# Reordering the ScalarE and VectorE work of pair 3 in the first MLP product

## The chip, the cores and the metric

The kernel is one program on one core of a Trainium2 chip, in float32 throughout (the matrix products are made of rounded parts, see below). The metric is the device time of one execution in microseconds (us), lower is better. The engines are called as in the profile: PE (TensorE), ACT (ScalarE), DVE (VectorE), POOL (GpSimd) and SP (SyncE, which only issues transfers here). Each engine works through its own list of instructions in the order in which the program gives them, and waits at a semaphore until it has reached the number asked for.

## The reference, cut to what matters

The reference is one layer of a diffusion trunk: a norm, a combined projection, a mixer, an output projection, and then an MLP, over 1024 tokens of width 1024. The change touches only the MLP's first product and its squared ReLU:

```python
D_MODEL = 1024
D_FF = 4 * D_MODEL
h2 = modulate(x, norm2_w, sh2, sc2)
return x + g2 * (jnp.square(jax.nn.relu(h2 @ w_mlp1)) @ w_mlp2)
```

## The kernel before, in words

**The tiling.** The 4096 hidden features are 32 tiles of 128, taken two at a time as 16 pairs, 0 to 15. Pairs 0 and 1 are multiplied plainly. From pair 2 on a pair is a 2 by 2 block product, two rows of 128 features by two halves of 512 tokens, with the contraction cut in two, and is made with 7 block products in place of 8. Weights and activations are combined by sums and differences before, and the results after. Each block product is 12 matmuls of 128x128 by 128x512: four tiles of the contraction, each with rounded weights by rounded activations, rounded weights by the rest of the activations, and the rest of the weights by rounded activations.

**PE.** `hidden_products(i, odd)` makes the seven products of pair i in the order `HID_ORDER = (0, 5, 2, 1, 4, 3, 6)`. I call them product 1 to product 7 of the pair by their place in this order. They go into three PSUM accumulators: A (in `ob`), B and C (in `sm`). Product 1 fills A. Product 3 goes on adding to A, so the content of A has to be copied out before it (first copy). Product 5 adds to A again (second copy before it). Product 4 begins C anew, and product 6 adds to C (third copy between them). Product 7 adds to A after DVE's second addition has read it.

**ACT, the weight parts.** `w1_high(pair, n, b)` writes the rounded weights for product n+1 of the pair, one 128x512 instruction at L1882 (`slot<-raw` or `slot<-held`); `held` and two quarters of `raw` come from POOL's sums.

**DVE, the weight parts.** `w1_low(pair, n, b)` subtracts the rounded weights from the exact ones (L2534), and PE waits for it at each product.

**POOL.** `part_sums1` makes four sums for each pair (L889, L891, L894, L897), each held up by a count of `w1_low`: the fourth one, L897, of the pair waits until `w1_low(pair, 3)` is done, since it overwrites `held`, and the first one, L889, of the next pair waits for `w1_low(pair, 5)`.

**The way out of the banks.** `copy_out(i, odd, n, ...)` on ACT (L1941) copies an accumulator to the buffer `hid`. `add_out` on DVE (L2596) adds another accumulator to what was copied: the first addition adds B, the second adds A after product 5, and `third_out` adds C after product 6 and applies the squared ReLU. On ACT, `first_out` and `next_out` make the squared ReLU (L1910 and L1912) behind the first and second addition, and `last_block` makes it from A after product 7.

**The staged parts for the second product.** The squared hidden blocks of a pair are combined by DVE (`t_made`, L2568 to L2582, four of them in a row of dependences), rounded by ACT (`t_high`, L1936, seven for each pair), their rest made by DVE (`t_low`, L2589, seven for each pair), and stored to HBM by SP (`keep_hidden`, L709). Stage buffers are used again by the next pair, so `t_high` waits for the store of the pair before.

**What sets the order.** The order is written out by hand. Pair 2, and the staged parts of pairs 0 and 1, are a straight list ahead of the function `period(i, odd, kind)`, which is the list for one pair from 3 to 15, on ACT and on DVE. Within it, work of pair i (weight parts, copies, additions) is mixed with the staged parts of pair i-1. Only `period(3, 1)` is touched by the change; pairs 4 to 13 are a loop over the same function.

The semaphores that the prediction speaks of: `hid_prod` counts PE's products, `y_copied` the copies, `y_added` the additions, `w1_lo` the weight rests. PE's waits ahead of a product are these:

```python
if j in (2, 4, 3):
    pe.wait_ge(y_copied, i * 3 + {2: -5, 4: -4, 3: -3}[j])
if j == 6:
    pe.wait_ge(y_added, i * 3 - 4)
```

Of the kernel before, what the change touches and what calls it, by code (L numbers as in the profile page):

```python
# [64 lines left out]
NPART = 7  # L65
# [141 lines left out]
def hybrid_trunk(nc, wstream, wg_in, wm1, wm2, xt, ct, small_in, gw_in, out):  # L207
    ctx = ExitStack()
    with ctx:
# [1277 lines left out]
        def _(act):  # L1487
# [426 lines left out]
            def last_block(pair, odd):  # L1914

                act.wait_ge(hid_prod, pair * NPART - NPART)
                relu_squared(odd, 1, 0, pair * 3 - 3, hid_bank(ACC_A, odd))
# [20 lines left out]
            def copy_out(i, odd, n, acc, at, row, half):  # L1938

                act.wait_ge(hid_prod, i * NPART + (at + 1 - 2 * NPART))  # L1940
                act.activation(hid_block(odd, row, half), hid_bank(acc, odd), ACT.Copy).then_inc(y_copied, 1)  # L1941

            def first_out(i, odd):
                act.wait_ge(y_added, i * 3 - 5)
                relu_squared(odd, 0, 0, i * 3 - 5)

            def next_out(i, odd):
                act.wait_ge(y_added, i * 3 - 4)
                relu_squared(odd, 1, 1, i * 3 - 4)
# [27 lines left out]
            t_high(0, 0, 6, "first")  # L1977
            w1_high(2, 5, 0, True)
            w1_high(2, 6, 0, True)
            for j in T_ORDER[:2]:  # L1980
                t_high(1, 1, j, "plain")
            first_out(2, 0)
            act.wait_ge(t_lo, NPART)
            copy_out(2, 0, 1, ACC_A, 2, 0, 1)
            copy_out(2, 0, 2, ACC_C, 3, 1, 1)
            w1_high(3, 0, 1)
            w1_high(3, 1, 1)
# [1 line left out]
            t_high(1, 1, 2, "plain")  # L1989
            t_high(1, 1, 5, "plain")  # L1990
            t_high(1, 1, 4, "plain")
            t_high(1, 1, 6, "plain")
            next_out(2, 0)
            for j in T_ORDER[:2]:
                t_high(2, 0, j)

            def period(i, odd, kind=""):

                prev, old, new = i - 1, 1 - odd, 1 - odd
                last = kind == "last"  # L2000
                w1_high(i, 2, odd)
                last_block(prev, old)
                act.wait_ge(t_sum, i * 4 - 7)
                act.wait_ge(t_lo, i * NPART + (T_AT[0] + 1 - 2 * NPART))
                copy_out(i, odd, 0, ACC_A, 0, 0, 0)
                w1_high(i, 3, odd)
                t_high(prev, old, 1)
                t_high(prev, old, 2)
                w1_high(i, 4, odd)
                t_high(prev, old, 5)  # L2010
                first_out(i, odd)
                act.wait_ge(t_lo, i * NPART + (T_AT[4] + 1 - 2 * NPART))
                copy_out(i, odd, 1, ACC_A, 2, 0, 1)
                w1_high(i, 5, odd)
                t_high(prev, old, 4)
                copy_out(i, odd, 2, ACC_C, 3, 1, 1)
                w1_high(i, 6, odd)
                t_high(prev, old, 6)
                if last:
                    w2_high(0, 0, 0, True)  # L2020
                    w2_high(0, 0, 1, True)
                else:
                    w1_high(i + 1, 0, new)
                next_out(i, odd)
                if not last:
                    w1_high(i + 1, 1, new)
                for j in T_ORDER[:2]:
                    t_high(i, odd, j, "last" if last else "")
                if last:
                    t_high(i, odd, 1, "last")  # L2030
                    w2_high(0, 0, 2, True)

            period(3, 1)
            with act.Fori(2, 7) as q:
                period(q * 2, 0)
                period(q * 2 + 1, 1)
# [57 lines left out]
        def _(dve):  # L2094
# [554 lines left out]
            t_made(1, 1, 4, "plain")  # L2649
            t_low(1, 1, 5)  # L2650
            t_low(1, 1, 4)
            t_low(1, 1, 6)
            third_out(2, 0)
            for j in T_ORDER[:2]:
# [2 lines left out]
            def period(i, odd, kind=""):  # L2657

                prev, old, new = i - 1, 1 - odd, 1 - odd
                last = kind == "last"  # L2660
                w1_low(i, 2, odd)
                for n in (1, 2, 3):
                    t_made(prev, old, n)
                w1_low(i, 3, odd)
                t_low(prev, old, 1)
                add_out(i, odd, 0, ACC_B, 1, 0, 0)
                w1_low(i, 4, odd)
                t_low(prev, old, 2)
                t_made(prev, old, 4)
                w1_low(i, 5, odd)  # L2670
                t_low(prev, old, 5)
                w1_low(i, 6, odd)
                t_low(prev, old, 4)
                add_out(i, odd, 1, ACC_A, 4, 1, 1)
                if last:
                    w2_low(0, 0, 0)
                else:
                    w1_low(i + 1, 0, new)
                t_low(prev, old, 6)
                third_out(i, odd)  # L2680
                if last:
                    t_low(i, odd, 0, kind)
                    t_made(i, odd, 1)
                    t_low(i, odd, 3, kind)
                else:
                    w1_low(i + 1, 1, new)
                    for j in T_ORDER[:2]:
                        t_low(i, odd, j)

            period(3, 1)  # L2690
            with dve.Fori(2, 7) as q:
                period(q * 2, 0)
                period(q * 2 + 1, 1)
# [180 lines left out]
```

## Time and profile before

| what | value |
|---|---|
| device time, median of 3 runs | 1073.67 us |
| lowest and highest of the 3 | 1072.82 and 1074.81 us |
| the profiled execution, device time | 1072.9 us |
| its span, first to last instruction | 1071.1 us |
| PE busy in the span | 1051.0 us, 98% |
| DVE busy in the span | 812.7 us, 76% |
| mean granted TensorE clock | 0.997 of full speed |

The span is 1.8 us shorter than the time of the same execution. Busy shares are means over the whole program; the stretch that the change touches is about 40 us long, from 480 to 521 us after the span's start. A row of the timeline gives the start, the duration, the engine, the source line, the operation and its tiles, how many instructions are merged in the row, and in brackets how long the engine had been idle before it and what ended that.

### The profile page before, as it was taken

To read this page: it belongs to the slowest core of one execution; us is meant where nothing else is said; L and a number is where in the kernel's file an instruction comes from. 1 tells how busy PE (TensorE), PEld (TensorE's weight loads), DVE (VectorE), ACT (ScalarE), POOL (GpSimd) and SP (SyncE) were. 2 spreads that over 40 slices of the span, in tenths; PEclk is the share of its full clock that TensorE was granted. 3 is DMA by queue.
4 is the path that set the end of the run, shared out by engine and by line. 5 is a ranking of instruction groups with operands and counts; after the bars stand their busy time and mean duration, and the time that the engine had idled before them with its cause. 6 is when DMAs were issued, how large, how long until landed. Compare 5 with 4: busy or idle time off the path is not lost.

```text
span 1071.1 us, 16432 instructions
## 1 busy us (share of the span) xinstructions
PE 1051.0 (98%) x5566; PEld 849.9 (79%) x5566; DVE 812.7 (76%) x1069; ACT 515.3 (48%) x833; POOL 273.6 (26%) x268
## 2 busy tenths in 40 slices
PE   7999999999999999999999999999999999999996
PEld 4688888777788888887888888888788888888884
DVE  5878868656546864899887787878988777787776
ACT  6665444357526233676667666666422222222234
POOL 1000006586101000012423323233422231222223
PEclk9999999999999999999999999999999999999998
DMA  9623331101013871226876675768755854774604
GB/s 350 254 90 127 118 118 40 41 21 40 28 53 117 308 278 62 79 98 249 321 265 246 232 272 222 273 235 307 302 192 202 352 219 176 311 282 177 246 1 157
DMA packets 66646, 199.82 MB, mean 187 GB/s; under 512 B 5664, under 2 KB 15136, under 8 KB 66592
## 3 DMA queue, kind: packets, MB, share of 16 engines
q1 hardware_dynamic: 66592, 199.11, 49.3%
q8 instruction: 33, 0.54, 0.2%
q14 instruction: 21, 0.17, 0.0%
HBM read 139.32 MB, written 59.77 MB: 186 GB/s over the span
## 4 chain that ended last, share of the span: by engine, by line
PE 48%; DVE 5%; DMA 1%; issue 1%; ACT 0%; POOL 0%; SPq 0%; DVEq 0%; ACTq 0%; POOLq 0%
PE main L1457 13%; PE ob L1415 12%; PE sm L1415 9%; PE sm L1457 8%; PE ob L1457 6%; DVE stage L2589 1%; DMA hidden_kept<-stage 1%; DVE XR L2707 1%; DVE XR L2779 1%; DVE slot L2539 0%; DVE slot L2534 0%; DVE t_tmp L2573 0%; DVE stage_last L2589 0%; DVE hid L2596 0%; DVE h_sum L2545 0%
## 5 line engine op out<-in xcount | busy, mean ns | idle before, releaser
L1415 PE MATMUL ob<-h_sum,slot 128*128 128x512 f32 x504 | 121.5, 390 | 2.3 <-ACT hid L1941 1.8
L957 PE MATMUL main<-a_hi,w_hi 128*128 128x512 f32 x376 | 123.0, 408 | 0.0
L1894 ACT ACTIVATE slot<-raw 128x512 fp32r<-128x512 f32 x80 | 50.1, 631 | 148.5 <-PE main L1457 58.4
L957 PE MATMUL main<-a_lo,w_hi 128*128 128x512 f32 x376 | 116.4, 391 | 0.0
L957 PE MATMUL main<-a_hi,w_lo 128*128 128x512 f32 x376 | 116.1, 390 | 0.0
L1415 PEld LDWEIGHTS ob<-h_sum,slot 128*128 128x128 f32 x504 | 94.3, 188 | 23.1 <-DVE slot L2534 2.9
L2707 DVE SCALAR_TENSOR_TENSOR XR<-main,small,XR 128x512 f32<-128x512 f32 x112 | 83.3, 750 | 28.8 <-PE main L1457 27.7
L957 PEld LDWEIGHTS main<-a_lo,w_hi 128*128 128x128 f32 x376 | 70.6, 188 | 15.5
L957 PEld LDWEIGHTS main<-a_hi,w_lo 128*128 128x128 f32 x376 | 70.6, 188 | 15.3
L957 PEld LDWEIGHTS main<-a_hi,w_hi 128*128 128x128 f32 x376 | 67.0, 188 | 15.8 <-issue 2.9
L1457 PE MATMUL main<-t_even,slot 128*128 128x512 f32 x336 | 78.1, 389 | 0.0
L2534 DVE TENSOR_TENSOR slot<-raw,slot 128x512 fp32r<-128x512 f32 x70 | 62.9, 900 | 17.6 <-ACT slot L1882 17.6
L1415 PE MATMUL sm<-h_hi,slot 128*128 128x512 f32 x224 | 73.5, 389 | 0.0
L1457 PEld LDWEIGHTS main<-t_even,slot 128*128 128x128 f32 x336 | 63.1, 188 | 13.1
L889 POOL TENSOR_TENSOR held<-raw 128x512 f32<-128x512 f32 x14 | 23.0, 1642 | 183.5 <-DMA raw<-wstream 136.2
L838 POOL TENSOR_TENSOR scaled_state<-tst,decay 64x128 f32<-64x128 f32 x60 | 28.5, 475 | 144.6 <-ACT tst L1623 140.1
L2539 DVE TENSOR_TENSOR slot<-raw,slot 128x512 fp32r<-128x512 f32 x80 | 59.8, 763 | 1.9 <-ACT slot L1894 1.9
L2707 DVE SCALAR_TENSOR_TENSOR XR<-sm,small,XR 128x512 f32<-128x512 f32 x64 | 47.7, 748 | 13.0 <-PE sm L1457 12.1
L1894 ACT ACTIVATE slot<-part_sum 128x512 fp32r<-128x512 f32 x32 | 20.2, 631 | 64.4 <-POOL part_sum L921 29.2
L918 POOL TENSOR_TENSOR raw<-part_sum,raw 128x512 f32<-128x512 f32 x16 | 21.3, 1332 | 115.2 <-DVE slot L2539 115.2
L2707 DVE SCALAR_TENSOR_TENSOR XR<-ob,small,XR 128x512 f32<-128x512 f32 x48 | 35.7, 749 | 17.8 <-PE ob L1457 17.7
L1415 PEld LDWEIGHTS sm<-h_hi,slot 128*128 128x128 f32 x224 | 42.0, 188 | 8.7
(341 smaller groups left out, 2401.6 us busy)
## 6 DMA issues: line engine op xcount, KB each, us to landing
hidden_kept<-stage SPq DMA_DIRECT2D x98, 512.0 KB, 4.5
raw<-wstream SPq DMA_DIRECT2D x60, 512.0 KB, 4.3
t_even<-hidden_kept SPq DMA_DIRECT2D x56, 512.0 KB, 5.5
raw<-wstream SPq DMA_DIRECT2D x16, 1024.0 KB, 5.7
stage<-hidden_kept SPq DMA_DIRECT2D x21, 512.0 KB, 5.1
stage_last<-hidden_kept SPq DMA_DIRECT2D x21, 512.0 KB, 6.0
wmod<-wm SPq DMA_DIRECT2D x8, 1024.0 KB, 11.7
mbuf<-wm SPq DMA_DIRECT2D x16, 512.0 KB, 4.1
```

Source lines behind the costliest of these rows:

```text
L838: pool.tensor_tensor(scaled_state[DK:P, :], tst[DK:P, h % 2, c, :], decay[DK:P, h, c:c + 1].broadcast_to([DK, DV]), ALU.mult).then_inc(sta ...
L889: pool.tensor_tensor(sums, a21, a22, ALU.add).then_inc(w1_sum, 1)
L918: pool.tensor_tensor(a11, sums, a11, ALU.subtract).then_inc(w2_sum, 1)
L957: ins = pe.matmul(main[:, bank, half * HALF:(half + 1) * HALF], w[:, slot, k, :], x[:, half * HALF:(half + 1) * HALF], start=begin, stop=end)
L1415: ins = pe.matmul(hid_bank(acc, odd), slots1[j][:, w, kp, :], parts[x][:, kp, :], start=PARTS[j][3] and kp == 0 and m == 0, stop=kp == KP ...
L1457: ins = pe.matmul(product_bank(s, acc, q), slots2[j][:, w, q, kp, :], tset[odd][j][kp][:, x, :], start=begins and kp == 0 and n == 0, stop ...
L1894: act.activation(slots2[j][:, 0, :, :, :], operand(s, j), ACT.Copy).then_inc(w2_hi, 1)
L2534: tt(slots1[j][:, 1, :, :], operand1(b, j), slots1[j][:, 0, :, :].bitcast(F32), ALU.subtract).then_inc(w1_lo, 1)
L2539: tt(slots2[j][:, 1, :, :, :], operand(s, j), slots2[j][:, 0, :, :, :].bitcast(F32), ALU.subtract).then_inc(w2_lo, 1)
L2589: tt(y[:, 1, :], sources(odd)[j], y[:, 0, :].bitcast(F32), ALU.subtract).then_inc(t_lo, 1)
L2707: stt(out=XR[m][:, cols], in0=product_bank(s, acc, q), scalar=mods[:, 3, m:m + 1], in1=XR[m][:, cols], op0=ALU.mult, op1=ALU.add).then_inc ...
L2779: stt(out=XR[k][:, cols], in0=bank(4 + n), scalar=one_col("fw", k), in1=XR[k][:, cols], op0=ALU.mult, op1=ALU.mult).then_inc(out_made, 1)
```

## The change

On ACT, in the list for pair 2, the second copy of pair 2 goes ahead of one staged part and of `first_out(2)`. Still ahead of `period(3, 1)`, the third and fourth weight parts of pair 3 and its first copy are put in: the third weight part ahead of the last staged part of pair 1, the first copy ahead of `next_out(2)`, the fourth weight part ahead of the first staged parts of pair 2. In `period(3, 1, "begun")` the fifth weight part and the second copy of pair 3 stand directly behind `last_block`, ahead of three staged parts and `first_out(3)`.

On DVE, the third weight rest of pair 3 goes ahead of the last staged rest of pair 1. Within the period the fourth and fifth weight rests each stand where the third and fourth stood. The weight rest for product 1 of pair 4 moves ahead of a staged rest and of pair 3's second addition. PE, POOL and SP have the same lists as before. All other pairs keep their order. No instruction is added or taken away.

```diff
             w1_high(2, 6, 0, True)
-            for j in T_ORDER[:2]:
-                t_high(1, 1, j, "plain")
-            first_out(2, 0)
+            t_high(1, 1, T_ORDER[0], "plain")
             act.wait_ge(t_lo, NPART)
             copy_out(2, 0, 1, ACC_A, 2, 0, 1)
+            t_high(1, 1, T_ORDER[1], "plain")
+            first_out(2, 0)
             copy_out(2, 0, 2, ACC_C, 3, 1, 1)
...
             t_high(1, 1, 4, "plain")
+            w1_high(3, 2, 1)
             t_high(1, 1, 6, "plain")
+            act.wait_ge(t_sum, 5)
+            act.wait_ge(t_lo, NPART + T_AT[0] + 1)
+            copy_out(3, 1, 0, ACC_A, 0, 0, 0)
             next_out(2, 0)
+            w1_high(3, 3, 1)
             for j in T_ORDER[:2]:
                 t_high(2, 0, j)
...
+                if kind == "begun":
+                    last_block(prev, old)
+                    w1_high(i, 4, odd)
+                    second_copy()
+                    t_high(prev, old, 1)
+                    t_high(prev, old, 2)
+                    t_high(prev, old, 5)
+                    first_out(i, odd)
...
-            period(3, 1)
+            period(3, 1, "begun")
...
             t_low(1, 1, 4)
+            w1_low(3, 2, 1)
             t_low(1, 1, 6)
...
-                w1_low(i, 2, odd)
+                begun = kind == "begun"
+                w1_low(i, 3 if begun else 2, odd)
                 for n in (1, 2, 3):
                     t_made(prev, old, n)
-                w1_low(i, 3, odd)
+                w1_low(i, 4 if begun else 3, odd)
                 t_low(prev, old, 1)
                 add_out(i, odd, 0, ACC_B, 1, 0, 0)
-                w1_low(i, 4, odd)
+                if not begun:
+                    w1_low(i, 4, odd)
...
                 w1_low(i, 6, odd)
+                if begun:
+                    w1_low(i + 1, 0, new)
                 t_low(prev, old, 4)
                 add_out(i, odd, 1, ACC_A, 4, 1, 1)
```

The order on ACT from the last staged parts of pair 1 to the first addition's squared ReLU of pair 3, before. `slot1_2`, `slot1_1`, `slot1_4` are the third, fourth and fifth weight part, `hid1<-ob` at L1941 is the first copy and then the second, `stage` are staged parts.

```order
L1936 ACTIVATE stage6_161<-t_tmp_140 128x512
L1910 ACTIVATE hid0_134<-hid0_134 128x512
L1912 ACTIVATE hid0_134<-hid0_134 128x512
L1936 ACTIVATE stage0_155<-hid0_134 128x512
L1936 ACTIVATE stage3_158<-hid0_134 128x512
L1882 ACTIVATE slot1_2_143<-raw1_1_192 128x512
L1910 ACTIVATE hid0_134<-ob 128x512
L1912 ACTIVATE hid0_134<-hid0_134 128x512
L1941 ACTIVATE hid1_135<-ob 128x512
L1882 ACTIVATE slot1_1_142<-held_137 128x512
```

The same place on ACT with the change, up to the second copy:

```order
L1882 ACTIVATE slot1_2_143<-raw1_1_192 128x512
L1936 ACTIVATE stage6_161<-t_tmp_140 128x512
L1941 ACTIVATE hid1_135<-ob 128x512
L1910 ACTIVATE hid0_134<-hid0_134 128x512
L1912 ACTIVATE hid0_134<-hid0_134 128x512
L1882 ACTIVATE slot1_1_142<-held_137 128x512
L1936 ACTIVATE stage0_155<-hid0_134 128x512
L1936 ACTIVATE stage3_158<-hid0_134 128x512
L1910 ACTIVATE hid0_134<-ob 128x512
L1912 ACTIVATE hid0_134<-hid0_134 128x512
L1882 ACTIVATE slot1_4_145<-raw1_1_192 128x512
L1941 ACTIVATE hid1_135<-ob 128x512
```

The first copy (first L1941 row of each) had eight of these instructions ahead of it and has two now, the last staged part of pair 1 and the third weight part. The second copy (last row) stands ahead of the staged parts 1, 2 and 5 of pair 2, which it followed before.

The order on DVE in the period of pair 3, before, from the fourth weight rest to the second addition. `hid1<-hid1,sm` is the first addition, `hid1<-hid1,ob` the second, `slot1_0<-raw1_0` the first weight rest of pair 4.

```order
L2534 TENSOR_TENSOR slot1_1_142<-held_137,slot1_1_142 128x512
L2589 TENSOR_TENSOR stage1_156<-t_tmp_140,stage1_156 128x512
L2596 TENSOR_TENSOR hid1_135<-hid1_135,sm 128x512
L2534 TENSOR_TENSOR slot1_4_145<-raw1_1_192,slot1_4_145 128x512
L2589 TENSOR_TENSOR stage2_157<-t_tmp_140,stage2_157 128x512
L2582 TENSOR_TENSOR t_tmp_140<-hid0_134,t_tmp_140 128x512
L2534 TENSOR_TENSOR slot1_3_144<-held_137,slot1_3_144 128x512
L2589 TENSOR_TENSOR stage5_160<-hid0_134,stage5_160 128x512
L2534 TENSOR_TENSOR slot1_6_147<-raw1_1_192,slot1_6_147 128x512
L2589 TENSOR_TENSOR stage4_159<-hid0_134,stage4_159 128x512
L2596 TENSOR_TENSOR hid1_135<-hid1_135,ob 128x512
L2534 TENSOR_TENSOR slot1_0_141<-raw1_0_191,slot1_0_141 128x512
```

The same place on DVE with the change, from the fifth weight rest (L2552 is the weight rests' line there, L2607 the staged rests', L2614 the additions', L2600 the fourth difference's):

```order
L2552 TENSOR_TENSOR slot1_4_145<-raw1_1_192,slot1_4_145 128x512
L2607 TENSOR_TENSOR stage1_156<-t_tmp_140,stage1_156 128x512
L2614 TENSOR_TENSOR hid1_135<-hid1_135,sm 128x512
L2607 TENSOR_TENSOR stage2_157<-t_tmp_140,stage2_157 128x512
L2600 TENSOR_TENSOR t_tmp_140<-hid0_134,t_tmp_140 128x512
L2552 TENSOR_TENSOR slot1_3_144<-held_137,slot1_3_144 128x512
L2607 TENSOR_TENSOR stage5_160<-hid0_134,stage5_160 128x512
L2552 TENSOR_TENSOR slot1_6_147<-raw1_1_192,slot1_6_147 128x512
L2552 TENSOR_TENSOR slot1_0_141<-raw1_0_191,slot1_0_141 128x512
L2607 TENSOR_TENSOR stage4_159<-hid0_134,stage4_159 128x512
L2614 TENSOR_TENSOR hid1_135<-hid1_135,ob 128x512
```

All three weight rests `slot1_2`, `slot1_1` and `slot1_4` now stand ahead of the first addition, where two of them stood; ahead of the second addition the first weight rest of pair 4 has come in.

## Rows read from the trace of the kernel before

**Rows 1.** The page's busy time (share of the span) and instructions, two engines.

```profile
PE 1051.0 (98%) x5566; PEld 849.9 (79%) x5566; DVE 812.7 (76%) x1069; ACT 515.3 (48%) x833; POOL 273.6 (26%) x268
```

**Rows 2.** Busy time by stretch: start:end us, length, engines' busy time, clock, DMA.

```profile
core 0: us, PE busy (x) PEld busy (x) DVE busy (x) ACT busy (x) POOL busy (x), PEclk, DMA share, GB/s
479.92:499.56 19.64, 19.30 (x86) 15.69 (x85) 19.61 (x23) 12.38 (x22) 7.66 (x4) 1.00 0.53 214
499.56:521.00 21.44, 19.52 (x85) 15.45 (x84) 20.64 (x31) 16.39 (x31) 6.60 (x4) 1.00 0.91 323
521.00:540.04 19.04, 19.04 (x86) 15.77 (x85) 15.82 (x25) 13.27 (x25) 6.33 (x4) 1.00 0.76 273
```

**Rows 3.** Timeline of PE, pairs 3 and 4: starts of products.

```profile
502.27 0.39 PE L1415 MATMUL sm<-h_hi,slot 128*128 128x512 f32 x1
...
506.92 3.00 PE L1415 MATMUL ob<-h_sum,slot 128*128 128x512 f32 x12 [1.76 <-ACT hid L1941]
...
518.28 3.00 PE L1415 MATMUL ob<-h_sum,slot 128*128 128x512 f32 x12 [0.16 <-DVE hid L2596]
...
529.28 2.88 PE L1415 MATMUL sm<-h_sum,slot 128*128 128x512 f32 x12
```

**Rows 4.** The chain of work that ended last, in pair 3: start, us, what.

```profile
504.01 8.94 DMA hidden_kept<-stage
...
517.54 0.61 DVE hid L2596
```

**Rows 5.** Timeline of ACT, pair 3 and one row of pair 4.

```profile
501.76 0.64 ACT L1936 ACTIVATE stage<-t_tmp 128x512 fp32r<-128x512 f32 x1 [1.33 <-DVE t_tmp L2582]
...
506.19 0.58 ACT L1941 ACTIVATE hid<-ob 128x512 f32<-128x512 f32 x1
...
510.50 0.63 ACT L1910 ACTIVATE hid<-hid 128x512 f32<-128x512 f32 x1 [0.73 <-DVE hid L2596]
...
511.71 0.58 ACT L1941 ACTIVATE hid<-ob 128x512 f32<-128x512 f32 x1
512.19 0.62 ACT L1882 ACTIVATE slot<-held 128x512 fp32r<-128x512 f32 x1
513.02 0.63 ACT L1936 ACTIVATE stage<-hid 128x512 fp32r<-128x512 f32 x1 [0.22 <-DMA hidden_kept<-stage]
...
529.48 0.60 ACT L1941 ACTIVATE hid<-ob 128x512 f32<-128x512 f32 x1 [0.60 <-PE ob L1415]
```

**Rows 6.** Timeline of DVE, pair 3.

```profile
505.98 0.69 DVE L2534 TENSOR_TENSOR slot<-raw,slot 128x512 fp32r<-128x512 f32 x1
...
507.37 0.69 DVE L2573 TENSOR_TENSOR t_tmp<-hid,t_tmp 128x512 f32<-128x512 f32 x1
...
508.58 0.68 DVE L2534 TENSOR_TENSOR slot<-held,slot 128x512 fp32r<-128x512 f32 x1
...
509.79 0.68 DVE L2596 TENSOR_TENSOR hid<-hid,sm 128x512 f32<-128x512 f32 x1
510.38 1.19 DVE L2534 TENSOR_TENSOR slot<-raw,slot 128x512 fp32r<-128x512 f32 x1
...
512.84 0.69 DVE L2534 TENSOR_TENSOR slot<-held,slot 128x512 fp32r<-128x512 f32 x1
...
514.70 1.14 DVE L2534 TENSOR_TENSOR slot<-raw,slot 128x512 fp32r<-128x512 f32 x1 [0.56 <-ACT slot L1882]
515.76 1.78 DVE L2589 TENSOR_TENSOR stage<-hid,stage 128x512 fp32r<-128x512 f32 x1
517.46 0.68 DVE L2596 TENSOR_TENSOR hid<-hid,ob 128x512 f32<-128x512 f32 x1
```

**Rows 7.** Timeline of POOL, the sums of pairs 3 and 4.

```profile
509.41 1.61 POOL L897 TENSOR_TENSOR held<-raw 128x512 f32<-128x512 f32 x1 [11.25 <-DVE slot L2534]
513.61 1.68 POOL L889 TENSOR_TENSOR held<-raw 128x512 f32<-128x512 f32 x1 [2.58 <-DVE slot L2534]
515.36 1.63 POOL L891 TENSOR_TENSOR raw<-raw 128x512 f32<-128x512 f32 x1
```

More of the change, by code:

```diff
@@ L2000, in period, with second_copy @@
                 last = kind == "last"
[L2001 to L2013, printed above, removed]
+                def second_copy():
+                    act.wait_ge(t_lo, i * NPART + (T_AT[4] + 1 - 2 * NPART))
+                    copy_out(i, odd, 1, ACC_A, 2, 0, 1)
+                if kind == "begun":
[6 more added lines that the diff above has]
+                    first_out(i, odd)
+                else:
+                    w1_high(i, 2, odd)
+                    last_block(prev, old)
+                    act.wait_ge(t_sum, i * 4 - 7)
+                    act.wait_ge(t_lo, i * NPART + (T_AT[0] + 1 - 2 * NPART))
+                    copy_out(i, odd, 0, ACC_A, 0, 0, 0)
+                    w1_high(i, 3, odd)
+                    t_high(prev, old, 1)
+                    t_high(prev, old, 2)
+                    w1_high(i, 4, odd)
+                    t_high(prev, old, 5)
+                    first_out(i, odd)
+                    second_copy()
                 w1_high(i, 5, odd)
@@ L2676, in period @@
                     w2_low(0, 0, 0)
-                else:
+                elif not begun:
                     w1_low(i + 1, 0, new)
@@ L2688, in period @@
                         t_low(i, odd, j)
-            period(3, 1)
+            period(3, 1, "begun")
             with dve.Fori(2, 7) as q:
```

## The prediction

> **What bounds the kernel now.** I read the page's busy times first: PE is busy for 98% of the span and DVE for 76% [rows 1]. So almost all time is PE's, and a reordering can only win back PE's idle time in the stretch that it touches. Then I cut that stretch by pairs. Pair 2 takes 19.64 us, pair 3 takes 21.44 us, and pair 4, which stands for all later ones, takes 19.04 us with PE busy throughout [rows 2]. Pair 3 loses 2.40 us against pair 4. The reader is also to see DVE in the same rows: busy 19.61 of 19.64 us and 20.64 of 21.44 us, against 15.82 of 19.04 in pair 4. In pairs 2 and 3 DVE is as full as PE.
>
> The timeline of PE says where the 2.40 us lie. A product takes 19.04 / 7 = 2.72 us [rows 2]. Product 2 starts at 502.27, so product 3 could start at 504.99; it starts at 506.92 and names ACT's copy out of the bank, 1.93 us late. From there four products take 10.88 us, so product 7 could start at 517.80; it starts at 518.28 and names DVE's second addition, another 0.48 us [rows 3]. The sum is 2.41 us. The chain of waits has no copy at 506 us in it. It goes back from product 7 to the addition at 517.54 on DVE, and through staged parts to a store to HBM that landed after 8.94 us [rows 4]. The first gap is therefore not what sets the end of pair 3; without it PE would come to product 7 earlier and find DVE's addition not there.
>
> **The first copy.** It starts at 506.19 on ACT. With the change it stands behind the staged part that starts at 501.76 [rows 5] and needs product 1, which is done when product 2 starts at 502.27. From a product's end to a copy takes about 0.20 us: product 3 of pair 4 ends at 529.28, where the next starts, and the copy begins at 529.48 [rows 3, 5]. So it runs from about 502.5 to 503.1 and product 3 starts at 504.99. The wait of 1.93 us is gone, and products 3 and 4 take PE to 510.43. I take the step to do what its code says.
>
> **DVE up to the first addition.** Successive 128x512 operations on DVE start 0.60 us apart: 509.79 to 510.38 [rows 6]. The first addition starts at 509.79 and has two weight rests of pair 3 ahead of it; now it has three, +0.60 us. A second term comes from POOL. L897 waits for the fourth weight rest, which takes the third's place one operation later: 505.98 + 0.60 = 506.58, done after 0.68 at 507.26. In the trace L897 starts at 509.41 and ends at 511.02 [rows 7], and the DVE operation issued at 510.38 takes 1.19 us and ends at 511.57, 0.55 after POOL's end, while the addition from `sm` beside it takes its usual 0.68 [rows 6]. So an operation on two SBUF blocks waits for POOL's end and then needs 0.55 more. Now L897 starts at about 507.41 (0.15 behind the rest, as before, where the rest ended at 509.26) and ends 1.61 later at 509.02. The second difference, at 507.37 before and 507.97 now, ends at 509.57 in place of 508.66: +0.91 us. This stall existed before too, but it fell behind the first addition and partly under one that reads PSUM. Now it falls ahead. The first addition starts at 509.79 + 0.60 + 0.91 = 511.30 and ends at 511.98.
>
> The Trainium skill (SBUF — State Buffer, "SBUF: two separate sides") says that POOL and a DVE instruction with two SBUF inputs take one port pair in turn, each for a whole instruction. It speaks against this change, and the rows agree: 1.19 us beside L897, 0.68 us with a PSUM input. Without such a lock the 0.91 would be nothing and the sum below +0.7 us; with it, +1.6 us.
>
> **ACT behind the first addition.** `first_out` waits for that addition, and the sixth weight part is queued behind it on ACT. Before: the addition ends at 510.47, ACT starts at 510.50, and the weight part at 512.19, with the second copy between. The copy (511.71 to 512.19, 0.48 us) has come ahead and is no longer between: 511.98 + 0.03, and 1.21 for relu and square (510.50 to 511.71), gives 513.22 for the weight part [rows 5]. DVE's sixth weight rest follows 0.65 behind it (512.19 to 512.84), at 513.87: +1.03 us. The second copy itself waits for product 3 (ends 507.71), starts at 507.9, and holds three staged parts back to 508.4; DVE reads the first of them only at about 510.7, so this costs nothing. Product 5 needs the fifth weight rest, which is done at about 510.8, and the second copy, done long before. Product 6 needs the sixth rest (514.6) and the third copy. The staged part ahead of the third copy waited 0.22 us for its store at 513.02 [rows 5]; the store's issue is unmoved, and ACT now comes there at 513.7, so it is covered, with 0.7 us to spare. The third copy ends near 514.8, and product 6 starts near 515.0, ends at 517.7.
>
> **DVE up to the second addition.** From the sixth weight rest to the second addition took 517.46 - 512.84 = 4.62 us [rows 6], with L889 at 513.61 and L891 at 515.36 in it, both started by that same rest [rows 7]. They move with it, and so do their two stalls (the rows of 1.14 and 1.78 us). Added is the first weight rest of pair 4, +0.60 us. DVE's idle 0.56 us at 514.70 gives nothing back: that operation ended at 515.84, 0.55 behind L889's end, so it was POOL that held it, and L889 moves too. The second addition starts at 513.87 + 4.62 + 0.60 = 519.09 and product 7 0.82 us behind that (517.46 to 518.28), at 519.91.
>
> **The sum.** Product 7 of pair 3 moves from 518.28 to 519.91: 0.60 + 0.91 - 0.48 + 0.60 = +1.63. Of this the removed wait gives back nothing, since PE now waits about 0.4 us ahead of product 5, 1.4 ahead of product 6 and 2.2 ahead of product 7, 4.0 in all against 2.4. Pair 4 has slack: DVE is idle for 3.2 us there [rows 2]. I work its second weight rest out at 522.1 to 522.8 against a need at 525.4, and its first copy at 525.9 against 528.2. So nothing more is added and nothing is won back. In pair 2 the second copy comes 1.7 us sooner, but the weight rest that product 5 also waits for is unmoved on a DVE without idle time: nothing.
>
> The profiled execution took 1072.9 us against a span of 1071.1; so 1074.5 for it. The median of the runs shown is 1073.67, 0.8 above it, and I forecast 1073.67 + 1.6 = 1075.3 us, +0.15%. A measurement of this kernel tells about 0.2% (2.1 us) from no change, and the forecast lies within it, on the slow side.
>
> **The rivals.** (a) The delay on DVE is hidden: L897 falls between operations and costs nothing ahead of the addition. Without the 0.91 the sum is +0.7, and with ACT's `first_out` early enough that DVE waits nowhere, the added 0.60 alone remains, 1073.7 to 1074.4 us. For it: the stalls by POOL depend on tenths of a microsecond. Against it: L897 is released by DVE's own rest, and the next DVE operation that reads PSUM is the sixth behind it.
>
> (b) The change does what its words say and keeps it: the 1.93 us ahead of product 3 are won, product 7 starts at 516.35 and the time is 1071.7 us. It decides at the start of the second addition: before 517.46 there is a gain, and the whole one needs 515.5. DVE has 0.56 us of idle time at that place and more work than before, so this needs operations shorter than any row shows. At most half of it could pass 0.2%.
>
> (c) Slower by more: a store lands late. The stage part before the third copy waits for the store that took 8.94 us in a stretch with the DMA engines 91% busy [rows 2, 4]. Once it lands more than 0.7 us later than now, the third copy, the last weight parts and the second addition all go with it; 1 to 2 us more give +2.6 to +3.6, 1076.3 to 1077.3 us. ACT held by the second copy for product 3 belongs to the same case, if product 3 is late. For it: the row. Against it: the stores that compete are, if anything, issued later.
>
> **How the numbers follow.** The forecast 0.60 (its own range +0.7 to +2.4, so 1074.4 to 1076.1), (a) 0.20, (b) 0.05, (c) 0.15. The range leaves out (b) and the outer part of (c), and takes in that the median of three runs moved by about 0.5 us: 1073.2 to 1077.0. Slower by over 0.2% holds (c) and a fifth of the forecast, 0.15 + 0.12 = 0.27. Faster by over 0.2% is 0.03, from (b). The rest is 0.70.
>
> **What would show it.** In the new profile PE's wait for ACT's copy ahead of product 3 is gone, and PE waits for DVE's weight rests and second addition at products 5 to 7. L897 starts near 507.4, and a difference on DVE beside it takes about 1.6 us. The first addition starts near 511.3, the second near 519.1, product 7 near 519.9, and from then on PE has no gap. A first addition at 510.4 means (a); a staged part that waits on `hidden_kept<-stage` for more than a few tenths means (c); a product 7 before 518.28 refutes the sum.

## The result, and the profile after

The changed kernel takes 1074.92 us (median of 22 runs, 1073.75 to 1077.33), the kernel before 1073.09 us beside it (22 runs, 1072.21 to 1074.81). The ratio is 1.0018, 95% interval 1.0012 to 1.0023. By the ratio that is 1.9 us slower (1.3 to 2.5). The interval leaves out no change, but the size is at the edge of the 0.2% below which I call a difference none. The forecast was 1.6 us slower, 1075.3 us. Both kernels have a few longer runs: 8 of the 22 with the change took 1075.83 us or more, and 5 of the 22 before took 1074.17 or more.

The profiled execution has a span of 1072.6 us, against 1071.1. The stretches of pairs 2, 3 and 4 again (length, busy times of the engines, granted clock, DMA share), cut at PE's first matmul of each pair, to set beside [rows 2]:

```profile
core 0: us, PE busy (x) PEld busy (x) DVE busy (x) ACT busy (x) POOL busy (x), PEclk, DMA share, GB/s
479.80:498.83 19.03, 19.03 (x85) 15.76 (x84) 18.93 (x22) 11.89 (x21) 7.67 (x4) 1.00 0.54 221
498.83:522.65 23.82, 20.20 (x86) 15.46 (x84) 22.74 (x33) 17.10 (x32) 6.58 (x4) 1.00 0.90 331
522.65:541.69 19.04, 19.04 (x86) 15.77 (x84) 15.38 (x24) 13.16 (x24) 6.34 (x4) 1.00 0.60 227
```

One cut of [rows 2] is not at a first matmul: it is at 521.00, and pair 4's first matmul starts at 521.12. Pair 3 took 21.56 us before, cut as here. Pair 2 has lost its idle time (19.64 us before, 19.03 now), pair 3 has become longer by 2.26 us (21.56 to 23.82), pair 4 is as before (19.04). PE's products of pair 3, beside [rows 3]:

```profile
504.27 2.88 PE L1415 MATMUL ob<-h_sum,slot 128*128 128x512 f32 x12
507.23 3.01 PE L1415 MATMUL sm<-h_sum,slot 128*128 128x512 f32 x12
510.75 3.06 PE L1415 MATMUL ob<-h_sum,slot 128*128 128x512 f32 x12 [0.50 <-DVE slot L2552]
514.89 0.47 PE L1415 MATMUL sm<-h_hi,slot 128*128 128x512 f32 x1 [1.09 <-ACT hid L1941]
...
519.83 2.98 PE L1415 MATMUL ob<-h_sum,slot 128*128 128x512 f32 x12 [1.95 <-DVE hid L2614]
```

Product 3 no longer waits for the first copy: it starts at 504.27 in place of 506.92. But products 5, 6 and 7 wait now, 0.50, 1.09 and 1.95 us by the brackets, and product 7 starts at 519.83, against 518.28 before. The wait removed early in the pair has come back later in it, since what is ahead of product 7 is on DVE.

DVE with the change, from the fourth weight rest (beside [rows 6]; L2552 are weight rests, L2614 additions, L2591 the second difference):

```profile
506.49 0.68 DVE L2552 TENSOR_TENSOR slot<-held,slot 128x512 fp32r<-128x512 f32 x1
507.09 0.68 DVE L2586 TENSOR_TENSOR t_tmp<-hid 128x512 f32<-128x512 f32 x1
507.88 1.61 DVE L2591 TENSOR_TENSOR t_tmp<-hid,t_tmp 128x512 f32<-128x512 f32 x1
...
510.01 0.68 DVE L2552 TENSOR_TENSOR slot<-raw,slot 128x512 fp32r<-128x512 f32 x1
...
511.22 0.67 DVE L2614 TENSOR_TENSOR hid<-hid,sm 128x512 f32<-128x512 f32 x1
...
513.78 0.69 DVE L2552 TENSOR_TENSOR slot<-held,slot 128x512 fp32r<-128x512 f32 x1 [0.68 <-ACT slot L1882]
...
515.30 3.18 DVE L2552 TENSOR_TENSOR slot<-raw,slot 128x512 fp32r<-128x512 f32 x2 [0.23 <-ACT slot L1882]
518.40 0.68 DVE L2607 TENSOR_TENSOR stage<-hid,stage 128x512 fp32r<-128x512 f32 x1
519.01 0.67 DVE L2614 TENSOR_TENSOR hid<-hid,ob 128x512 f32<-128x512 f32 x1
```

POOL's sums there, beside [rows 7]:

```profile
507.32 1.62 POOL L897 TENSOR_TENSOR held<-raw 128x512 f32<-128x512 f32 x1 [9.24 <-DVE slot L2552]
514.55 1.68 POOL L889 TENSOR_TENSOR held<-raw 128x512 f32<-128x512 f32 x1 [5.61 <-DVE slot L2552]
516.31 1.63 POOL L891 TENSOR_TENSOR raw<-raw 128x512 f32<-128x512 f32 x1
```

L897 starts at 507.32 and the difference beside it takes 1.61 us. The first addition stands at 511.22 (forecast 511.30), the sixth weight rest at 513.78 (513.87), the second addition at 519.01 (519.09).

### The profile page after: what moved, and what is told of

It reads as the page before. It is cut to its first block, busy times and chain, and to the rows that moved or that the text cites. A ratio compares the mean times of both kernels' runs of the same rounds, so it can differ in the third digit from the quotient of the medians.

```text
span 1072.6 us, 16432 instructions
## 1 busy us (share of the span) xinstructions
PE 1051.2 (98%) x5566; PEld 849.9 (79%) x5566; DVE 813.0 (76%) x1069; ACT 515.5 (48%) x833; POOL 274.5 (26%) x268
## 4 chain that ended last, share of the span: by engine, by line
PE 89%; DVE 5%; POOL 2%; issue 1%; ACT 1%; DMA 1%; SPq 0%; DVEq 0%; POOLq 0%; ACTq 0%
PE main L957 25%; PE ob L1415 13%; PE main L1457 13%; PE sm L1415 10%; PE sm L1457 8%; PE ob L1457 6%; PE main L975 2%; PE main L1348 2%; PE main L1207 2%; PE main L1381 1%; PE ob L1381 1%; DMA xs<-xt 1%; DVE XR L2730 1%; PE ob L1159 1%; POOL scaled_state L838 1%
## 5 line engine op out<-in xcount | busy, mean ns | idle before, releaser
L2552 DVE TENSOR_TENSOR slot<-raw,slot 128x512 fp32r<-128x512 f32 x70 | 64.1, 917 | 17.2 <-ACT slot L1882 17.2
L889 POOL TENSOR_TENSOR held<-raw 128x512 f32<-128x512 f32 x14 | 24.2, 1728 | 188.3 <-DMA raw<-wstream 136.2
```

The source lines that it names most:

```text
L889: pool.tensor_tensor(sums, a21, a22, ALU.add).then_inc(w1_sum, 1)
L2552: tt(slots1[j][:, 1, :, :], operand1(b, j), slots1[j][:, 0, :, :].bitcast(F32), ALU.subtract).then_inc(w1_lo, 1)
```

## The experiments

Executions differ by up to 2 us in what happens ahead of 480 us (e1_w40_back below), so times in pair 3 are compared as a distance: from DVE's fourth difference of pair 1 (L2582 before, L2600 with the change), which ends a stretch in which DVE has next to no idle time, to PE's product 7 of pair 3. I call it the distance. The fourth difference before and with the change:

```profile
501.04 0.68 DVE L2582 TENSOR_TENSOR t_tmp<-hid,t_tmp 128x512 f32<-128x512 f32 x1
```

```profile
500.96 0.68 DVE L2600 TENSOR_TENSOR t_tmp<-hid,t_tmp 128x512 f32<-128x512 f32 x1
```

The distance is 518.28 - 501.04 = 17.24 us before and 519.83 - 500.96 = 18.87 us with the change, +1.63. Three profiles of the changed kernel gave 18.87, 18.87 and 18.86 us; every other kernel here has one profile. Theory 1 is the prediction's: DVE's list ahead of its two additions, with POOL's stalls in it, sets product 7. Its rivals were that ACT's new order or a late store sets it. The ratios of the first four experiments stand beside the change's 1.0018 (1.0012 to 1.0023); their intervals overlap it, so these experiments rest on the distance.

**One operation less ahead of the second addition (e1_w40_back).**

```diff
-                if begun:
-                    w1_low(i + 1, 0, new)
                 t_low(prev, old, 4)
                 add_out(i, odd, 1, ACC_A, 4, 1, 1)
                 if last:
                     w2_low(0, 0, 0)
-                elif not begun:
+                else:
                     w1_low(i + 1, 0, new)
```

> The changed kernel, but the first weight rest of pair 4 stands behind pair 3's second addition on DVE again, as before. Theory 1 (DVE's list ahead of its two additions sets product 7 of pair 3): one operation fewer ahead of the second addition, so that starts 0.60 us earlier, at 518.4, and product 7 at 519.2 in place of 519.83; in time 0.6 us less than the changed kernel. Theory 2 (the end of pair 3 is set by ACT's new order, or by a store that lands late, through the third copy): product 7 stays at 519.8.

Measured: the difference at 502.83, product 7 at 521.09, distance 18.26 us: 0.61 less than with the change. Time 1073.83 us, ratio to before 1.0007 (0.9998 to 1.0016). Its times in the span are all later by some 1.9 us, from ahead of pair 2, and this is why the absolute times in the expectation do not fit while the distance does. PE in this run, and its granted clock (the last but two of the numbers) early in the program, where it was 1.00 in the profile of the change:

```profile
521.09 2.98 PE L1415 MATMUL ob<-h_sum,slot 128*128 128x512 f32 x12 [1.35 <-DVE hid L2614]
```

```profile
24.00:26.00 2.00, 2.00 (x17) 0.97 (x13) 1.42 (x3) 2.00 (x4) 0.15 (x1) 0.53 1.07 385
28.00:30.00 2.00, 2.00 (x9) 0.71 (x11) 2.00 (x2) 0.00 (x0) 0.00 (x0) 0.50 1.12 395
```

The 0.60 term stands.

**One operation less ahead of the first addition (e2_w34_back).**

```diff
-                w1_low(i, 4 if begun else 3, odd)
+                if not begun:
+                    w1_low(i, 3, odd)
                 t_low(prev, old, 1)
                 add_out(i, odd, 0, ACC_B, 1, 0, 0)
-                if not begun:
-                    w1_low(i, 4, odd)
+                w1_low(i, 4, odd)
```

> The changed kernel, but the fifth weight rest of pair 3 stands behind the first addition on DVE. Theory 1: the first addition moves from 511.22 to 510.6, the sixth weight rest from 513.78 to 513.2, and product 7 from 519.83 to 519.2, although product 5 starts 1.2 us later than in the changed kernel (about 512.0), since its rest is late. Theory 2: the first addition is earlier but product 7 stays at 519.8. Theory 3 (PE's own lateness at product 5 carries on to the end): product 7 later than 519.83.

PE in this run:

```profile
512.40 3.02 PE L1415 MATMUL ob<-h_sum,slot 128*128 128x512 f32 x12 [1.69 <-DVE slot L2552]
519.67 2.97 PE L1415 MATMUL ob<-h_sum,slot 128*128 128x512 f32 x12 [1.53 <-DVE hid L2614]
```

Product 5 waits 1.69 us in place of 0.50, and still the distance is 519.67 - 501.42 = 18.25 us, 0.62 less. Time 1073.41 us, ratio 1.0008 (0.9999 to 1.0018). The longer wait on PE at product 5 cost nothing here, where product 7 waits for DVE, and theory 3 of the expectation falls.

**POOL's fourth sum kept off (e3_l897_late).**

```diff
+                if late:
+                    pool.wait_ge(y_added, 4)
                 pool.tensor_tensor(sums, a12, a11, ALU.subtract).then_inc(w1_sum, 1)
...
-            part_sums1(3, 1)
+            part_sums1(3, 1, late=True)
```

> The changed kernel, but POOL's fourth sum of pair 3 (L897) waits in addition for the first addition on DVE. Theory 1: the second difference on DVE takes 0.69 us in place of 1.61, and the first addition starts at 510.3, 0.9 us earlier. The stall comes back behind it (a difference or a staged rest held up until about 513.2, and the sixth weight part waits for the sum until 512.8), so that the sixth weight rest starts at 513.4 in place of 513.78 and product 7 at 519.4 to 519.5, 0.35 us less. If POOL's sum did not hold DVE, the first addition would stay at 511.2.

DVE and POOL in this run (lines stand two further down):

```profile
508.02 0.69 DVE L2593 TENSOR_TENSOR t_tmp<-hid,t_tmp 128x512 f32<-128x512 f32 x1
...
510.44 0.68 DVE L2616 TENSOR_TENSOR hid<-hid,sm 128x512 f32<-128x512 f32 x1
511.04 0.69 DVE L2609 TENSOR_TENSOR stage<-t_tmp,stage 128x512 fp32r<-128x512 f32 x1
511.64 1.79 DVE L2602 TENSOR_TENSOR t_tmp<-hid,t_tmp 128x512 f32<-128x512 f32 x1
```

```profile
511.29 1.59 POOL L899 TENSOR_TENSOR held<-raw 128x512 f32<-128x512 f32 x1 [13.07 <-DVE hid L2616]
```

The second difference takes 0.69 us in place of 1.61, and the fourth, now beside POOL's sum, 1.79 in place of 0.68. The stall follows POOL. The first addition is 9.34 us behind the fourth difference of pair 1 (510.44 - 501.10), against 10.26 with the change (511.22 - 500.96): 0.92 us, the prediction's second term of 0.91. The distance is 519.63 - 501.10 = 18.53 us, 0.34 less than with the change, since the stall comes back ahead of the sixth weight rest. Time 1074.24 us, ratio 1.0017 (1.0008 to 1.0026).

**ACT's part alone (e4_act_only).** The changed kernel with the whole DVE list of before.

```diff
-            w1_low(3, 2, 1)
...
-                w1_low(i, 3 if begun else 2, odd)
+                w1_low(i, 2, odd)
                 for n in (1, 2, 3):
                     t_made(prev, old, n)
-                w1_low(i, 4 if begun else 3, odd)
+                w1_low(i, 3, odd)
...
-                if not begun:
-                    w1_low(i, 4, odd)
+                w1_low(i, 4, odd)
...
-                if begun:
-                    w1_low(i + 1, 0, new)
```

> Only ACT's part of the change, DVE's list as before. Theory 1: the first copy is early, but product 3 now waits for its weight rest (506.66) and starts near 506.8; DVE's additions stay where they were, product 7 at 518.2 to 518.3, and the time is that of the kernel before. Theory 2 (ACT's new order costs the time): product 7 near 519.8 and 1.5 us more than the kernel before.

This expectation of theory 1 failed, and theory 2's number (product 7 near 519.8) was not met either. The distance is 521.82 - 501.31 = 20.51 us, and the time 1075.56 us, ratio 1.0024 (1.0015 to 1.0034). PE, ACT and DVE say why:

```profile
507.36 4.60 PE L1415 MATMUL ob<-h_sum,slot 128*128 128x512 f32 x12 [2.36 <-DVE slot L2552]
```

```profile
512.05 0.60 ACT L1941 ACTIVATE hid<-ob 128x512 f32<-128x512 f32 x1 [4.50 <-PE ob L1415]
```

```profile
513.20 0.69 DVE L2607 TENSOR_TENSOR stage<-t_tmp,stage 128x512 fp32r<-128x512 f32 x1 [3.30 <-ACT stage L1936]
513.81 0.68 DVE L2614 TENSOR_TENSOR hid<-hid,sm 128x512 f32<-128x512 f32 x1
```

Product 3 waits 2.36 us for its weight rest, which DVE has late. On ACT the second copy waits for product 3, 4.50 us, with the staged parts of pair 2 behind it, and DVE waits 3.30 us for the first of these, with the first addition behind it. The prediction had this chain (product 3, copy, staged part, staged rest, addition) and found it free, which holds in the whole change, where product 3 is early. On top of it product 3 took 4.44 us (507.36 to 511.80) in place of 2.72. The granted clock (last but two) in stretches of 2 us:

```profile
506.00:508.00 2.00, 0.64 (x3) 0.56 (x4) 1.90 (x4) 1.52 (x3) 0.00 (x0) 1.00 0.93 219
508.00:510.00 2.00, 2.00 (x7) 1.52 (x6) 1.90 (x3) 0.00 (x0) 0.00 (x0) 0.52 0.89 266
510.00:512.00 2.00, 2.00 (x7) 1.60 (x6) 0.00 (x0) 0.00 (x0) 1.28 (x1) 0.63 1.03 422
512.00:514.00 2.00, 2.00 (x10) 1.62 (x9) 0.80 (x2) 1.95 (x4) 0.00 (x0) 1.00 1.01 416
```

0.52 is close to the lower of the two levels (1.2 of 2.4 GHz), and stands behind PE's 2.36 us of idling. The distance is 3.3 us above that of before. Of these I put 1.7 (4.44 - 2.72) down to the clock and the other 1.6 to the chain; this is an estimate, since no run has one without the other. The profiled execution took 0.9 us more than the median, so the clock need not have fallen in each.

**DVE's part alone (e5_dve_only).** The ACT list of before, the DVE list of the change; the cut is against the kernel before.

```diff
             t_low(1, 1, 4)
+            w1_low(3, 2, 1)
             t_low(1, 1, 6)
...
-                w1_low(i, 2, odd)
+                begun = kind == "begun"
+                w1_low(i, 3 if begun else 2, odd)
...
-                w1_low(i, 3, odd)
+                w1_low(i, 4 if begun else 3, odd)
...
+                if begun:
+                    w1_low(i + 1, 0, new)
```

> Only DVE's part of the change, ACT's list as before. Theory 1: the third weight rest of pair 3 now stands on DVE ahead of work that is ready, but its rounded part comes from ACT at 505.1 only; DVE stands idle for 2.4 us there, and all behind it on DVE is late by as much. Counted from the fourth difference of pair 1 on DVE (501.04 before, 500.96 with the change), product 7 of pair 3 starts 21.5 us later, against 17.24 before and 18.87 with the whole change; in time 3 to 5 us above the kernel before, and more if the granted clock drops behind a long gap on PE, as it did in the run with ACT's part alone. A theory by which only DVE's three moved operations count would give 18.9 and 1.6 us.

Time 1079.03 us, ratio 1.0059 (1.0046 to 1.0073), 6.5 us slower. DVE waits 2.24 us for the third weight part, and later for two more:

```profile
505.29 0.69 DVE L2534 TENSOR_TENSOR slot<-raw,slot 128x512 fp32r<-128x512 f32 x1 [2.24 <-ACT slot L1882]
...
513.23 0.69 DVE L2534 TENSOR_TENSOR slot<-raw,slot 128x512 fp32r<-128x512 f32 x1 [0.62 <-ACT slot L1882]
...
517.48 0.69 DVE L2534 TENSOR_TENSOR slot<-held,slot 128x512 fp32r<-128x512 f32 x1 [1.16 <-ACT slot L1882]
...
522.69 0.67 DVE L2596 TENSOR_TENSOR hid<-hid,ob 128x512 f32<-128x512 f32 x1
```

```profile
517.08 5.46 PE L1415 MATMUL ob<-h_sum,slot 128*128 128x512 f32 x12 [4.31 <-ACT hid L1941]
```

The second addition comes at 522.69, 21.5 us behind the fourth difference of pair 1 (501.17), where I had put product 7 itself, so DVE alone would give a distance of 22.3. PE comes later still, at 525.36, a distance of 24.19: product 5 waited 4.31 us for the second copy, which in ACT's old list stands behind `first_out`, and then took 5.25 us to product 6 (517.08 to 522.33) in place of 2.72, at a granted clock of 0.50. So the distance was missed by 2.7 us. The time is as the expectation has it: 6.5 us less the clock's 2.5 is 4.0, within its 3 to 5. The change's two parts are worse alone than together.

**Pair 2's second copy alone (e6_pair2_copy).**

```diff
-            for j in T_ORDER[:2]:
-                t_high(1, 1, j, "plain")
-            first_out(2, 0)
+            t_high(1, 1, T_ORDER[0], "plain")
             act.wait_ge(t_lo, NPART)
             copy_out(2, 0, 1, ACC_A, 2, 0, 1)
+            t_high(1, 1, T_ORDER[1], "plain")
+            first_out(2, 0)
```

> The kernel before, with one part of the change alone: the second copy of pair 2 ahead of one staged part and of first_out(2) on ACT. With the change product 5 of pair 2 no longer waits, although the prediction put that wait on DVE's weight rest. Expected: product 5 of pair 2 starts at once behind product 4, pair 3 starts 0.6 us earlier, and product 3 of pair 3 waits 0.6 us longer for the same copy, since ACT's and DVE's work ahead of it does not move. Product 7 stays at 17.2 us behind the fourth difference of pair 1, and the time is that of the kernel before. If the gain were kept, product 7 would be at 16.6 and the time 0.6 us less.

```profile
490.45 2.88 PE L1415 MATMUL ob<-h_sum,slot 128*128 128x512 f32 x12
...
506.39 3.00 PE L1415 MATMUL ob<-h_sum,slot 128*128 128x512 f32 x12 [2.19 <-ACT hid L1941]
...
517.75 2.99 PE L1415 MATMUL ob<-h_sum,slot 128*128 128x512 f32 x12
```

Product 5 of pair 2 has no wait, as expected, and pair 2 takes 19.04 us in place of 19.64. Product 3 of pair 3 waits 2.19 us in place of 1.76, 0.43 more where 0.6 was expected, and the distance is 517.75 - 500.53 = 17.22 us, unchanged. Ratio 1.0006 (0.9997 to 1.0016), which does not tell a change.

**The second addition ahead of one staged rest, in the kernel before (e7_before_add_first).**

```diff
-                t_low(prev, old, 4)
+                if kind != "begun":
+                    t_low(prev, old, 4)
                 add_out(i, odd, 1, ACC_A, 4, 1, 1)
+                if kind == "begun":
+                    t_low(prev, old, 4)
...
-            period(3, 1)
+            period(3, 1, "begun")
```

> The kernel before, with the second addition of pair 3 ahead of one staged rest (stage4) on DVE. Theory 1 (DVE's list ahead of the addition sets product 7): the addition reads PSUM, is not held by POOL's L891, and starts near 515.8 in place of 517.46; then PE is the bound and product 7 starts where product 6 ends, at 517.9, that is 16.9 us behind the fourth difference of pair 1 against 17.24 before; 0.3 to 0.4 us less than before. Theory 2: no change.

DVE's second addition and POOL's sum beside it:

```profile
515.46 0.68 DVE L2596 TENSOR_TENSOR hid<-hid,ob 128x512 f32<-128x512 f32 x1
```

```profile
515.06 1.63 POOL L891 TENSOR_TENSOR raw<-raw 128x512 f32<-128x512 f32 x1
```

The addition, which reads PSUM, takes 0.68 us beside L891. The distance is 517.69 - 500.75 = 16.94 us, 0.30 less, and product 7 starts without a wait. Ratio 1.0001 (0.9989 to 1.0012): too small a part for the times.

**The same in the changed kernel, with pair 4's weight rest put back (e8_after_add_first).**

```diff
+                if not begun:
+                    t_low(prev, old, 4)
+                add_out(i, odd, 1, ACC_A, 4, 1, 1)
                 if begun:
-                    w1_low(i + 1, 0, new)
-                t_low(prev, old, 4)
-                add_out(i, odd, 1, ACC_A, 4, 1, 1)
+                    t_low(prev, old, 4)
                 if last:
                     w2_low(0, 0, 0)
-                elif not begun:
+                else:
                     w1_low(i + 1, 0, new)
```

> The changed kernel, with the first weight rest of pair 4 and one staged rest (stage4) both behind the second addition on DVE. Theory 1: the second addition starts near 516.7 in place of 519.01, product 6 ends near 517.7, and product 7 starts there: 16.8 us behind the fourth difference of pair 1, against 18.87 with the change and 17.24 before. In time 2 us less than the changed kernel and 0.4 us less than before. Theory 2 (a late store or ACT sets the end): 18 or more.

```profile
517.47 0.68 DVE L2614 TENSOR_TENSOR hid<-hid,ob 128x512 f32<-128x512 f32 x1
```

```profile
518.49 2.88 PE L1415 MATMUL ob<-h_sum,slot 128*128 128x512 f32 x12
```

The distance is 518.49 - 501.75 = 16.74 us, 2.13 less than with the change. Time 1072.07 us, ratio to before 0.9994 (0.9985 to 1.0003). Two operations behind the addition in place of ahead of it take the whole loss away: 1.20 us of DVE's time, and the stall beside POOL's L891 (517.08 to 518.71), which the addition, reading PSUM, does not meet. Product 7 has no wait, so from here PE's own products are the bound. ACT's list is that of the change in this run, so it is not ACT's order that sets product 7 with the change.

**Pair 3's lists rebuilt (e9_rebuilt).** DVE's list for pair 3 is now this; on ACT the third copy stands ahead of the staged part that waits for a store, and both weight parts of pair 4 ahead of the last staged part.

```python
w1_low(i, 3, odd)
t_made(prev, old, 1)
t_made(prev, old, 2)
w1_low(i, 4, odd)
add_out(i, odd, 0, ACC_B, 1, 0, 0)
t_made(prev, old, 3)
t_low(prev, old, 1)
t_low(prev, old, 2)
w1_low(i, 5, odd)
t_low(prev, old, 5)
add_out(i, odd, 1, ACC_A, 4, 1, 1)
w1_low(i, 6, odd)
t_made(prev, old, 4)
w1_low(i + 1, 0, new)
t_low(prev, old, 4)
w1_low(i + 1, 1, new)
t_low(prev, old, 6)
third_out(i, odd)
...
```

> The changed kernel with pair 3's lists rebuilt by theory 1: on DVE both additions come ahead of work that nothing on PE waits for (the fifth weight rest and the first addition ahead of the third difference, the second addition ahead of the seventh weight rest, the fourth difference and the staged rests behind it, the two first weight rests of pair 4 between them); on ACT the third copy ahead of the staged part that waits for a store, and pair 4's weight parts ahead of the last staged part. Expected: product 3 starts without a wait, product 5 waits 0.2 us at most, product 6 near 0.4 us for its weight rest, product 7 none. Product 7 starts 15.1 to 15.3 us behind the fourth difference of pair 1, against 17.24 before, 18.87 with the change and 16.74 with the additions first; the time is 2 us below the kernel before (ratio 0.998). The rival, that the backlog on DVE then stops pair 4, gives gaps on PE at products 2 or 3 of pair 4 and a gain of 1 us or less.

```profile
504.90 2.88 PE L1415 MATMUL ob<-h_sum,slot 128*128 128x512 f32 x12
507.64 3.02 PE L1415 MATMUL sm<-h_sum,slot 128*128 128x512 f32 x12
510.54 3.06 PE L1415 MATMUL ob<-h_sum,slot 128*128 128x512 f32 x12
513.72 0.50 PE L1415 MATMUL sm<-h_hi,slot 128*128 128x512 f32 x1
...
516.57 2.88 PE L1415 MATMUL ob<-h_sum,slot 128*128 128x512 f32 x12
```

The distance is 516.57 - 501.36 = 15.21 us, and no product waits longer than half a microsecond. Pair 4 has no gap. Time 1071.18 us, ratio to before 0.998 (0.9971 to 0.9989): 1.5 us by the medians below the kernel before on the same chip (1072.68) where 2 were expected, and the lowest ratio here.

**The changed kernel's profile twice more (e10_after_again, e11_after_again).** The same kernel, unedited.

> The changed kernel once more, for its profile. Product 7 of pair 3 starts 18.9 us behind the fourth difference of pair 1 again. Its executions spread from 1073.75 to 1077.33 us; if a lower granted clock behind the 2 us gap ahead of product 7 makes the slow ones, a profiled execution above 1076 us shows product 7 with a clock near half for part of its 2.7 us.

> The same as the run before, a third profile of the changed kernel: 18.9 us, and in an execution above 1076 us a lower granted clock behind one of the gaps in pair 3.

They have product 7 at 519.57 and 519.59, distances of 18.87 and 18.86 us. Their times were 1074.16 and 1074.15 us, so the expectation's condition (above 1076 us) was not met, and its question stays open. In the profile of e1_w40_back, at 1075.65 us, the lower clock is at 24 to 31 us, far ahead of pair 3, so time lost to the clock need not lie in pair 3's gaps.

## Why the prediction was right

The sum was 0.60 + 0.91 - 0.48 + 0.60 = +1.63 us at product 7 of pair 3, and the distance grew by 1.63 us. Term by term:

- **What bounds pair 3.** The chain, not the named wait ahead of product 3, was the right guide. With that wait gone (in the change, e1, e2 and e3) nothing was won; with two operations behind the second addition everything was won back (e8). In the kernel before, only 0.32 of the prediction's 0.48 us at product 7 were a wait: product 6 started at 515.24 and was over at 517.96. e7, which takes that wait away, gains 0.30.
- **The first copy.** It runs at 502.21, 0.3 us earlier than worked out. Product 1 was done 0.7 us earlier, so the staged part ahead on ACT (501.67) set the copy. Product 3 starts at once.
- **One operation more ahead of the first addition, 0.60.** Shown by e2: 0.62.
- **POOL's stall ahead of it, 0.91.** Shown by e3: 0.92 at the first addition. At product 7 only 0.34 of it came off, since the stall came back behind that addition. The stall falls on the DVE operation on two SBUF blocks that starts beside L897: the second difference with the change (1.61 us), the fourth in e3 (1.79). By the port lock that the Trainium skill states (SBUF — State Buffer, "SBUF: two separate sides") an addition that reads PSUM goes free, and it does: 0.68 us beside L891 in e7 and in e8. Rival (a), which had these 0.91 us hidden, falls. The low end of (a)'s range, 1073.7, did not follow from its own text, which leaves +0.6 or +0.7 us.
- **ACT without the second copy in between, -0.48.** From the first addition's start to the sixth weight rest 513.78 - 511.22 = 2.56 us, against 512.84 - 509.79 = 3.05 before [rows 6]: -0.49. No run tests it alone.
- **One operation more ahead of the second addition, 0.60.** Shown by e1: 0.61. The two stalls by L889 and L891 moved along as said: the row of 3.18 us, two weight rests, ends 0.54 behind L891.
- **The store (rival c) and the gain (rival b).** The store did not delay anything: ACT's staged part at 513.65 has no wait for `hidden_kept<-stage`. And (b) would have had the second addition ahead of 517.46; it came at 519.01.
- **A step that failed, without effect on the time.** The prediction said that pair 2's second copy gives nothing because product 5 of pair 2 also waits for a weight rest, as its row names. The weight rest of product 5 was an earlier operation and long done; the row named the rest of product 6, which with the change starts at 491.04, behind product 5 (490.68). The wait was for the copy, and it went: pair 3 starts 0.6 us sooner (e6, and the change). The time still gained nothing, for the reason that the prediction gave for pair 3: DVE's additions did not move. So PE's lost time in pair 3 came to 4.78 us (23.82 - 19.04) in place of the 4.0 worked out: 1.42 and 2.22 ahead of products 6 and 7 as forecast (1.4 and 2.2), but 0.24 and 0.80 ahead of products 4 and 5 (forecast 0 and 0.4), which PE reached sooner than their weight rests, and 0.10 in product 7 itself.

The interval of the measured 1.9 us (1.3 to 2.5) holds the 1.6 forecast. That the distance came out to the hundredth is in part luck: the four terms measure 0.62, 0.92, -0.49 and 0.61. The absolute forecast, 1075.3 us, was 0.4 above the measured 1074.92, since it started from 1073.67, the median of three runs, where 22 give 1073.09. The chance of 0.27 for slower by over 0.2% was not small beside a result at 0.18%.

## What to carry to other kernels

When a wait on the busiest engine is taken away, follow the other engine that is full in the same stretch to its last hand-over: if that is no earlier, the wait comes back there, and work moved ahead of it is paid for (here in full, 0.6 us for each of two weight rests). In lists kept in order, put the operation that another engine waits for ahead of work that nobody waits for yet, and try the two engines' lists together; here each half of the change alone was worse than the whole. The distance from a fixed instruction to the one that ends the stretch came out within 0.01 us in three profiles of one kernel, whose whole times spread over 3.6 us in 22 runs.

## What the runs showed of the hardware that was not expected

PE's granted clock fell to 0.52 after 2.36 us without matmuls (e4_act_only; the next product took 4.44 us in place of 2.72) and to 0.50 after 4.31 us (e5_dve_only, 5.25 us). But it stayed at 1.00 after 1.76 us in the kernel before, 1.95 us in the changed one, 2.19 us in e6_pair2_copy and 2.54 us in e5_dve_only (product 3 of pair 3, which took 2.81 us). In e1_w40_back it was at 0.50 to 0.53 from 24 to 30 us, behind waits of 0.64 and 0.77 us, while the kernel before kept 1.00 behind waits of 1.08 and 0.87 us at the same place. So a wait on PE can cost more than itself, but its length alone does not say whether it will, and what does is not shown here. In the three profiles of the changed kernel the clock did not fall in pair 3.
